# Short convolution and MLP layer on one core: the two projections of the convolution in turns of seven block products, like the MLP

## The reference, cut to what matters

```
h = rmsnorm(x, mix_norm)                       # x: 512 tokens x 2048
b_gate, c_gate, v = split(h @ w_in, 3)         # w_in: 2048 x 6144
u = c_gate * v
y = causal convolution of u over the tokens, 3 taps, one filter per channel
x = x + (b_gate * y) @ w_out                   # w_out: 2048 x 2048
h = rmsnorm(x, mlp_norm)
x = x + relu(h @ w1) ** 2 @ w2                 # w1: 2048 x 8192, w2: 8192 x 2048
```

## Time and profile before

| | |
|---|---|
| time before, median of 3 runs | 1972.85 us (1972.36 to 1973.45) |
| the profiled execution's own time | 1973.64 us |
| its span | 1971.8 us, 23073 instructions |
| TensorE busy | 1958.0 us, 99% |
| VectorE busy | 1483.0 us, 75% |
| ScalarE busy | 858.2 us, 44% |
| conv part | to about 716 us |
| up turns | about 716 to 1355 us |
| down turns | about 1355 us to the end |

### The profile page before, as it was taken

The page is one execution under the profiler, slowest core; times in us unless marked ns, Lnnn a source line. Parts: engine busy times, 40 slices in busy tenths (PEclk is TensorE's granted clock), DMA queues, the critical chain, the costliest instruction groups (busy, mean ns, idle before and its releaser), DMA issues.

```text
span 1971.8 us, 23073 instructions
## 1 busy us (share of the span) xinstructions
PE 1958.0 (99%) x8778; PEld 1621.5 (82%) x8778; DVE 1483.0 (75%) x1496; ACT 858.2 (44%) x1002; POOL 75.4 (4%) x146
## 2 busy tenths in 40 slices
PE   8999999999999999999999999999999999999999
PEld 7888888888888888888888888888888888888887
DVE  6335354363453669999999999999899889878878
ACT  6222222222223546656657557575444433334332
POOL 0000000000000100101001011010000000000000
PEclk9999999999999999999999999999999999999999
DMA  5332323222223536667687586789988888887783
GB/s 193 107 107 85 107 85 107 87 105 88 104 93 121 192 111 231 270 250 293 253 321 288 216 323 259 280 327 361 364 341 334 347 319 302 321 329 294 278 330 125
DMA packets 98318, 445.93 MB, mean 226 GB/s; under 512 B 10800, under 2 KB 10800, under 8 KB 73776
## 3 DMA queue, kind: packets, MB, share of 16 engines
q1 hardware_dynamic: 78944, 375.42, 50.5%
q0 software_dynamic: 19136, 69.21, 8.7%
q10 hardware_dynamic: 144, 0.04, 0.0%
HBM read 371.24 MB, written 73.40 MB: 225 GB/s over the span
## 4 chain that ended last, share of the span: by engine, by line
PE 98%; DVE 1%; issue 0%; ACT 0%; DMA 0%; DVEq 0%; ACTq 0%
PE pair L1084 61%; PE pair L989 35%; PE pair L1097 1%; PE pair L1055 0%; DVE raw L793 0%; DVE ring L799 0%; DMA cols<-in_cols 0%; ACT ring L454 0%; DVE act L713 0%; ACT quads L400 0%; PE pair L1019 0%; DVE tmp L614 0%; PE pair L1025 0%; PE pair L1022 0%; ACT L381 0%
## 5 line engine op out<-in xcount | busy, mean ns | idle before, releaser
L1084 PE MATMUL pair<-ring,act 128*128 128x512 f32 x5376 | 1229.3, 390 | 0.1
L1084 PEld LDWEIGHTS pair<-ring,act 128*128 128x128 f32 x5376 | 1006.5, 188 | 208.7 <-DVE ring L799 0.9
L454 ACT ACTIVATE ring<-raw 128x1024 fp32r<-128x1024 f32 x448 | 474.7, 1061 | 565.7 <-PE pair L1084 406.4
L799 DVE TENSOR_TENSOR ring<-raw,ring 128x1024 fp32r<-128x1024 f32 x448 | 537.6, 1219 | 90.0 <-ACT ring L454 89.4
L599 DVE TENSOR_TENSOR w_lo<-w_raw,w_hi 128x512 fp32r<-128x512 f32 x256 | 175.5, 692 | 349.2 <-ACT w_hi L377 343.9
L377 ACT ACTIVATE w_hi<-w_raw 128x512 fp32r<-128x512 f32 x256 | 161.4, 631 | 475.0 <-PE pair L989 471.7
L793 DVE TENSOR_TENSOR raw<-raw 128x1024 f32<-128x1024 f32 x256 | 301.6, 1219 | 5.6
L989 PE MATMUL pair<-h_hi,w_lo 128*128 128x512 f32 x764 | 298.2, 390 | 0.0
L989 PE MATMUL pair<-h_hi,w_hi 128*128 128x512 f32 x764 | 297.5, 389 | 0.0
L989 PE MATMUL pair<-h_lo,w_hi 128*128 128x512 f32 x764 | 297.5, 389 | 0.0
L989 PEld LDWEIGHTS pair<-h_hi,w_lo 128*128 128x128 f32 x764 | 143.6, 188 | 30.6 <-issue 0.8
(11 more groups left out here) (89 smaller groups left out, 748.1 us busy)
## 6 DMA issues: line engine op xcount, KB each, us to landing
raw<-in_mlp SPq DMA_DIRECT2D x128, 1024.0 KB, 7.7
act<-spill SPq DMA_DIRECT2D x224, 512.0 KB, 6.5
w_raw<-in_weights SPq DMA_DIRECT2D x63, 1024.0 KB, 4.9
spill<-stage POOLq DMA_DIRECT2D x112, 512.0 KB, 8.4
act<-act_kept SPq DMA_DIRECT2D x84, 512.0 KB, 8.0
act_kept<-act POOLq DMA_DIRECT2D x12, 512.0 KB, 6.3
mixed<-turned POOLq DMA_DIRECT2D x16, 256.0 KB, 2.9
x<-mixed SPq DMA_DIRECT2D x8, 512.0 KB, 12.0
```

Of the source, the lines that this page charges most:

```text
L454: nc.scalar.activation(ring[g % RING][:, 0], raw[:, r, 2 * (s % 2):2 * (s % 2) + 2, :], ACT.Copy).then_inc(hi_ready, 1)
L799: nc.vector.tensor_tensor(ring[g % RING][:, 1], raw[:, RAW_OF[s // 2], 2 * (s % 2):2 * (s % 2) + 2, :], ring[g % RING][:, 0].bitcast(F32), ...
L1084: mm = nc.tensor.matmul(bank, stationary, moving, start=(opens and k == 0 and n == 0), stop=(closes and k == NT - 1 and n == 2))
```

## The change: what it does

The plain path of the conv part is taken out. The kernel now has 48 turns of one kind: 12 for w_in, 4 for w_out, 16 up, 16 down. All 48 form T1 to T4 on VectorE. In the combinations of weights and of activations some signs differ from before, with as many operations. The input is read in quarters of the transposed x (`load_x`), scaled by ScalarE (`scale_x`), and once more as tokens to get the mean square (`square_tokens`); the norm's factor is put on the results, by token.

The first 16 turns are eight pairs of three kinds. GATED (pairs 0, 1, 3, 4) makes c_gate and v of one block of 512 channels: VectorE multiplies them (`form_u`), TensorE turns the product (2 quarters), ScalarE does the first tap, VectorE the two others (`more_taps`). GATE (pairs 2 and 5) makes b_gate of two blocks: TensorE turns it (4 quarters) and VectorE multiplies it into y (`gate`). MIXED (pairs 6 and 7) is w_out: GpSimd adds x to sums in SBUF by accumulating transfers (`add_x`), the result goes to HBM (`put_mixed`) and is turned (4 quarters).

Four turns (0, 1, 13, 17) take activations that were split just before, straight into their place (`direct_hi`, `direct_form`, `direct_lo`); the others load them or keep them. Up to turn 15 a second turn of a pair, and the turn behind it, load five products' activations again (S2, L12, S3, S4, L22); from turn 16 three, as before. The first turns of w_out and of the up part (12 and 16) load all seven.

The core of the diff (left out: deleted code of the plain path, buffer places, semaphores, waits that only follow the new numbering, and the host's order of the weights):

```diff
+KINDS = (GATED, GATED, GATE, GATED, GATED, GATE, MIXED, MIXED) + (UP,) * 8
+
+GATED_BLOCK = {0: 0, 1: 2, 3: 1, 4: 3}
+Z0, Z1, MIX0, UP0 = 2, 5, 6, 8
+NQP = len(KINDS)
...
+TURNS = [0]
+for _kind in KINDS:
+    TURNS.append(TURNS[-1] + (2 if _kind == GATED else 4))
...
+DIRECT_OF = {Z1: 2, MIX0 + 1: 3}
+SET_PAIRS = [Z0, MIX0] + list(range(UP0, NQP))
+SPILL_SET = {q: n for n, q in enumerate(SET_PAIRS)}
+
+DIRECT_TURN = {0: 0, 1: 1, V_OUT + 1: 2, V_UP + 1: 3}
...
+DIRECT_SPLIT = {(0, 0): (0, 1), (0, 2): (0, 2), (0, 3): (0, 3), (0, 4): (0, 4), (0, 5): (0, 5), (0, 6): (0, 6),
+                (0, 9): (1, 0), (0, 10): (1, 1), (0, 11): (1, 2), (0, 12): (1, 3), (0, 13): (1, 4), (1, 1): (1, 5),
+                (1, 3): (1, 6)}
+DIRECT_FORM = {(0, 1): (0, 1), (0, 2): (0, 2), (0, 3): (0, 3),
+               (0, 9): (1, 0), (0, 10): (1, 1), (0, 11): (1, 2), (0, 12): (1, 3)}
...
+def shared(v):
+
+    return (S2, L12, S3, S4, L22) if v < V_UP else (S2, S4, L22)
+
+
+def loaded(v):
+
+    if v >= V_DOWN or v in (V_OUT, V_UP):
+        return PRODUCTS
+    return () if v in DIRECT_TURN else shared(v)
...
+            def add_x(q, name, place):
+
+                t, f = int(name[0]) - 1, int(name[1]) - 1
+                o = BW * (q - MIX0 + 2 * f)
+                pool.dma_start(place[:], x_v[:, 2 * t:2 * t + 2, o:o + BW], accum_op=ALU.add).then_inc(x_added[name], 16)
...
+                if v % 2 and KINDS[q] == MIXED:
+                    first, s1, _, _, s4, l22 = sums_of(q)
+                    pool.wait_ge(copied, 5 * q + 4)
+                    add_x(q, "12", s4)
+                    pool.wait_ge(copied, 5 * q + 5)
+                    add_x(q, "21", l22)
+                    pool.wait_ge(added, 12 * q + 1)
+                    add_x(q, "11", first)
+                    pool.wait_ge(added, 12 * q + 4)
+                    add_x(q, "22", s1)
...
+            def direct_hi(d, j):
+                v = (1, 1, V_OUT + 1, V_UP + 1)[d] if d else 0
+                quads_there(act, d, {L11: NT, L12: 4 * NT}.get(j, 3 * NT), {L11: 1, L12: 3}.get(j, 4))
+                if j in (S1, S2, S3, S4):
+                    act.wait_ge(act_formed, 4 * d + {S1: 1, S2: 2, S3: 3, S4: 4}[j])
...
+            act.wait_ge(cols_in, 16)
+            scale_x("L11")
+            direct_hi(0, L11)
             for v in range(NV):
...
+            def form_u(q, half):
+
+                first, s1, _, _, s4, l22 = sums_of(q)
+                o, other = ((first, s4), (l22, s1))[half]
+                dve.wait_ge(added, 12 * q + (11, 12)[half])
+                dve.wait_ge(norm_step, NORM_X)
+                for i in range(2):
+                    nc.vector.scalar_tensor_tensor(out=o[:, i, :], in0=o[:, i, :],
+                                                   scalar=rstd_sq[:, 2 * half + i:2 * half + i + 1], in1=other[:, i, :],
+                                                   op0=ALU.mult, op1=ALU.mult).then_inc(u_formed, 1)
+
+            def more_taps(q, i):
+                tile = NT * GATED_BLOCK[q] + i
+                done = 2 * (FORMED_U[q] + i)
+                o = (quads1, quads2)[GATED_BLOCK[q] // 2][:, :, i, :]
+                dve.wait_ge(y_first, FORMED_U[q] + i + 1)
+                for j in (1, 2):
+                    k = TAPS + DT * j + tile
+                    link(nc.vector.scalar_tensor_tensor(out=o, in0=u_pad[:, i, j:j + S].rearrange("p (a t) -> p a t", a=2),
+                                                        scalar=cols[:, k:k + 1], in1=o, op0=ALU.mult, op1=ALU.add),
+                         y_step, done + j)
+
+            def gate(q, m):
+                dve.wait_ge(quad_turned, TURNS[q] + m + 1)
+                dve.wait_ge(y_step, 2 * FORMED_U[q])
+                o = quad[("L11", "L22", "L12", "L21")[m]].rearrange("p a t -> p (a t)")
+                nc.vector.tensor_tensor(o, pairs[1][:].rearrange("p a t -> p (a t)"), o, ALU.mult).then_inc(quad_ready, 1)
...
+            direct_lo(0, L11)
             for v in range(NV):
...
-                u = v - UP
+                u = v - V_DOWN
                 for s in range(SLOTS):
                     split_turn_lo(v, s)
+                    if (v, s) == (0, 0):
+                        direct_form(0, 0)
                     if s == 1:
...
+                    if (v, s) in DIRECT_SPLIT:
+                        direct_lo(*DIRECT_SPLIT[v, s])
+                    if (v, s) in DIRECT_FORM:
+                        direct_form(*DIRECT_FORM[v, s])
...
+                        if KINDS[q - 1] == GATED:
+                            if s in (2, 3):
+                                form_u(q - 1, s - 2)
+                            if s in (10, 11, 12, 13):
+                                more_taps(q - 1, s - 10)
+                        if KINDS[q - 1] == GATE and s in (3, 5, 6, 7):
+                            gate(q - 1, {3: 0, 5: 1, 6: 2, 7: 3}[s])
...
-            for k in range(KT):
-                products(1, k, 1, H)
-            with pe_loop(1, OUT0 // 2) as two:
-                for sub in range(2):
-                    whole_block(2 * two + sub, sub, H)
-
...
+                        if 2 <= v <= V_DOWN and v % 2 == 0:
+                            at_slot = {4: 0, 5: 1} if KINDS[v // 2 - 1] == GATED else {0: 0, 2: 1, 4: 2, 5: 3}
+                            if s in at_slot:
+                                turn_quad(v // 2 - 1, at_slot[s])
```

More of the change, by code:

```diff
@@ L43 @@
 ROTATE = (S1, S2, S3, S4, L22)
-SHARED = (S2, S4, L22)
+GATED, GATE, MIXED, UP = range(4)
+KINDS = (GATED, GATED, GATE, GATED, GATED, GATE, MIXED, MIXED) + (UP,) * 8
+GATED_BLOCK = {0: 0, 1: 2, 3: 1, 4: 3}
+Z0, Z1, MIX0, UP0 = 2, 5, 6, 8
+NQP = len(KINDS)
+V_OUT, V_UP, V_DOWN = 2 * MIX0, 2 * UP0, 2 * NQP
+TURNS = [0]
+for _kind in KINDS:
+    TURNS.append(TURNS[-1] + (2 if _kind == GATED else 4))
+RECTIFIED = [8 * sum(k in (GATE, UP) for k in KINDS[:q]) for q in range(NQP + 1)]
+FORMED_U = [4 * sum(k == GATED for k in KINDS[:q]) for q in range(NQP + 1)]
@@ L66, in conv_mlp_layer, with loads @@
+def loaded(v):
+    if v >= V_DOWN or v in (V_OUT, V_UP):
+        return PRODUCTS
+    return () if v in DIRECT_TURN else shared(v)
+def loads(v, j):
+    return sum(j in loaded(w) for w in range(v + 1))
+KEPT = (5, 5, 5, 3)
+NORM_X, NORM_M = 6, 14
+def conv_mlp_layer(nc, xt, x, turns, cols_dram, out, FF):
     D, S = xt.shape
@@ new lines, in conv_mlp_layer @@
+        later = {"L11": later1[:, 0], "L21": later1[:, 1], "L12": later2[:, 0], "L22": later2[:, 1]}
+        ones = at("ones", MISC, [P, P])
+        eye = at("eye", MISC + 512, [P, P])
+        cols = at("cols", MISC + 1024, [P, (2 + CW) * DT])
+        junk = at("junk", MISC + 1344, [P, BW])
+        NORM = MISC + 1344 + 2 * KB
+        part, part2 = at("part", NORM, [P, NT]), at("part2", NORM + 32, [P, 4, NT])
+        var_t, root_t, rstd_x, rstd_sq, rstd_m = (at(n, NORM + 96 + 32 * i, [P, NT]) for i, n in enumerate(
+            ("var_t", "root_t", "rstd_x", "rstd_sq", "rstd_m")))
@@ L320, in _ @@
                         load_raw(after, r)
-                    if after == UP and j in (L11, S1, L12, S3):
+                    if v == 0 and r == R11:
+                        sp.wait_ge(act_lo_ready, NPROD)
+                        for t in (0, 1):
+                            load_tokens(t)
+                    if after == V_DOWN and j in (L11, S1, L12, S3):
                         product_done(sp, v, j)
@@ new lines, in take_mixed @@
+            def take_mixed(q, m):
+                act.wait_ge(quad_turned, TURNS[q] + m + 1)
+                quads_free(act, q)
+                f = (0, 1, 1, 0)[m]
+                for i in range(NT):
+                    tile = MLP + NT * (q - MIX0 + 2 * f) + i
+                    ins = nc.scalar.activation(quad[("L11", "L22", "L12", "L21")[m]][:, i, :], by_channels()[:, i, :],
+                                               ACT.Copy, scale=cols[:, tile:tile + 1])
+                ins.then_inc(quad_ready, 1)
@@ L910, in _ @@
[L910 to L921 removed]
+                            add_pair(q - 1, 12)
```

1086 lines of the change are left out of this document (423 added, 663 removed).

## The result

The changed kernel takes 1976.66 us (1975.9 to 1978.17), the kernel before, run beside it, 1972.89 (1972.27 to 1973.64): ratio 1.002, 95% interval 1.0013 to 1.0027. So there is no gain, and a loss of the size of what can be told from no change. The forecast was 1919.

A forecast was written before the change was run, and what follows sets the result against it. TensorE was taken as the bound, with VectorE barely keeping up. 148.6 us to turn 2's end, 1713.9 for 45 turns, 47.3 for transposes, 1.6 and 4.4 gave 1915.8; 3.2 added made 1919, range 1908 to 1930 (66%).

The forecast's parts named there:

- TensorE's work: All 48 turns: 8064 matmuls at 0.2267 us plus 448 transposes; work falls by 73.0 us.
- The accumulating transfers: MIXED pairs: cost 0 if landing within 17 us of issue; row of 8.4 us taken as nearest.
- The bound on the slow side: Accumulating transfers at three times the row: up to 8 us for two MIXED pairs.
- 5.9 of lead lie behind: MIXED pairs: cover for a late accumulating transfer, on top of 10.9 us before VectorE needs the last one.
- Start, turns 0 and 1, turn 2: First matmul at 12.2 us, turn 1 ends at 104.4, turn 2 at 148.6; 20.4 us of stalls behind the first matmul.
- Conv pair boundaries: Turns behind a GATE pair: the chain turned quarter, gate, next quarter comes 0.8 us late in two turns, 1.6 us.
- The "no lead" rival: First turns behind GATED have no lead; seven later conv pair boundaries each lose 4.3 us: +30, 1949; chance 13%.
- From turn 18: Up and down turns and the end: same order as before, 1175.1 us.
- The slow clock: Rival: gaps in turn 0 keep TensorE at 1.2 GHz, turn 0 is 18 us later; about 1933 to 1937; chance 8%.
- The rival on the slower side: MIXED pairs: accumulating transfers landing about 44 us after issue lose the 53 us won; 1985 at 50 us; chance 4%.
- The outcome near "same": Whole kernel: time within about 0.2% (4 us) of the one before; chance 0.01.
- the signs of being wrong: TensorE waiting over 3 us in a pair after turn 2, VectorE waiting for `x_added`, turn 0 matmuls 0.43 apart, up pair over 79.8.

The follow-up runs named there:

- e3: The whole changed kernel shifted by 32 bytes, so the ring stays 32 bytes off the activations' grid: 1976.78 us.
- e5: The changed kernel with its buffers placed anew, so that ring and activations are whole KB apart (distance 0): 1937.38 us.
- e6: The kernel before with its weight buffers and ring moved 32 bytes further, activations where they were: 2025.88 us.
- e9: e5 without the accumulating transfers of the two MIXED pairs and VectorE's waits for them, so x is not added: 1926.08 us.
- e14: e5 with VectorE's addition 4 ahead of addition 3, so a MIXED pair's last accumulating transfer is issued earlier: 1933.32 us.

## Why the prediction was wrong

- **TensorE's work, the step that failed.** 8064 + 448 instructions was right. "8064 matmuls x 0.2267" took a price over from the old layout; in the new one it is 0.2333. That is 53 us of work (e3, e5, e6). It shows as 39.3 us between the changed kernel and e5 (40.7 by the spans), since where VectorE or a transfer sets the end a faster TensorE only waits more: 7.9 of a possible 13 to turn 12, almost nothing in turns 12 to 17 (their time is set by the transfers and VectorE at either pace), and 32.3 from turn 18.
- **The accumulating transfers** were taken at 0 for up to about 17 us from issue, and cost 11 at 13 to 17 us. The length was near the far end of what was allowed for. (The bound on the slow side was also half of what it should be: at three times the row, 25.2 us, 8.4 are over in each of two pairs, 17 in all and not 8.) In pair 6 VectorE stood at the sum 8.8 us after the issue (13.3 - 4.5), where 10.9 had been counted. The cover was wrong: "5.9 of lead lie behind" counts the ring alone. In pair 7 the addition behind the late one also frees the bank that TensorE needs, and only the last of the four transfers had been looked at, where the third was late.
- **Start, turns 0 and 1, turn 2.** Forecast: first matmul at 12.2, turn 12 at 501.0. Measured in e5: 11.5 and 503.04. VectorE as the bound there, 61 instructions at 1.137, was sized rightly: it begins the rest of turn 1's slot 8 at 84.9 and is done by 86.1, forecast 88.1. By the count of matmuls turn 1 ends at 106.9 (104.4) and turn 2 at 146.8 (148.6); turns 3 to 11 then take 3.8 us more than their terms, so that the 503.04 is in part luck.
- **Conv pair boundaries.** TensorE's waits for gated quarters (`DVE quads L791`) are 1.8 us in three times in the kernel after; forecast 1.6 in two. The "no lead" rival wanted 4.3 us at each pair boundary; in e9 no gap of TensorE between turns 3 and 12 is over 1.2 us.
- **From turn 18.** Forecast 1175.1, measured 1176.05 in e5: at distance 0 the old rows carry over to a tenth of a per cent.
- **Rivals.** The slow clock came in part: the second slot already ran at the high level (3.06 us), the clock fell once in turn 0, at about 34 us (25 matmuls in 7.62 us), and again in turns 14 and 15. The first fall is hidden behind VectorE (turn 0 takes 52.0 us in e5 and 51.9 in e14, where the clock doesn't fall in it), the one in turn 15 of e5 costs about 2 us. The Trainium skill ("TensorE: Matmul & The Clock Gate", HAM oscillation) describes pauses for data that are longer than the work between them, and a fall at each. The gaps in turn 0 of the kernel after are 0.6 to 2.9 us, shorter than the slots, and only the last of the four is followed by a fall, so neither "each time" nor "never" fits. The rival on the slower side named the transfers, which were too short for it (17 us, not 44). The outcome near "same" came from a cause that stood in none. Of the signs of being wrong, three came: an up pair takes 81.9 us in the kernel after (785.65 to 867.51 in its chain), VectorE waits for `x_added`, and TensorE waits over 3 us in a MIXED pair.

The line with `+ 32` stood in the change, and the working put no price on it. No row of before could have shown one, as all its matmuls of weights have distance 0. But "the same instruction" had been taken for granted for the one term that was 95% of the sum, without a bound from both sides; everything that got such bounds was about a hundredth of it.

The Trainium skill ("SBUF — State Buffer", Operand start alignment) asks of an operand's start only that it is a multiple of the element's size, and says that this is about legality, not speed. All distances here keep to that, and they differ by 2.9% in pace.

## What to carry to other kernels

Where a rewrite places buffers anew, the largest term's unit price is not a constant: compare the pace of a long row of matmuls (its time over its number in the chain of waits) before reading any wait. Keep stationary and moving operands of such float32r matmuls at the same address modulo 256 bytes, and put odd-sized buffers last. When an engine is made faster, ask which stretches it bounds, since only there the gain arrives; and count as cover the thing that is freed last, here a result bank and not the ring.

## What the runs showed of the hardware

- A float32r matmul of 128 x 512 takes 0.2267 us in a row of many where moving and stationary operand have the same address modulo 256 bytes, 0.2333 at 32, 96, 192 and 224, 0.2324 at 128, 0.2289 at 64. Shifting both together by 32 changes nothing.
- The length of a matmul's own row hardly tells (397 ns on average after, about 390 before); the distance between rows does.
- A transfer of 512 KB from HBM that is added to SBUF landed after 11.5 to 13.7 us in the median, the same as a plain load after 6.5 to 9.9.
- The granted clock of TensorE fell to its lower level behind short gaps as well: at about 34 us in the kernel after, where none had been over 2.9 us since the first matmul, and in e5 in the 4.94 us that it stood idle at 665 to 670 us.
